# Stick-breaking attention on one Trainium2 core: the values as stationary operand in two column tiles, the output row turned back by one product

## What is computed

```
# SB_HEADS = 8, SB_DIM = 64, SEQ = 2048, Q_BLOCK = 128
def stick_breaking_block(q, k, v, q_pos, k_pos):
    z = jnp.einsum('bhtd,bhsd->bhts', q, k).astype(jnp.float32) * (SB_DIM ** -0.5)
    mask = k_pos[None, :] < q_pos[:, None]
    log_beta = jnp.where(mask, jax.nn.log_sigmoid(z), -jnp.inf)
    log_1m = jnp.where(mask, jax.nn.log_sigmoid(-z), 0.0)
    rest = lax.cumsum(log_1m, axis=3, reverse=True) - log_1m
    a = jnp.exp(log_beta + rest)
    return jnp.einsum('bhts,bhsd->bhtd', a.astype(v.dtype), v)
```

## Time and profile before

| | |
|---|---|
| median of 3 runs | 3280.84 us (3278.66 to 3281.20) |
| profiled execution: its own time | 3281.12 us |
| profiled execution: span from first to last instruction | 3279.5 us |
| PE busy, share of the span | 3177.8 us, 97% |
| DVE / ACT / POOL busy | 1542.3 / 1075.8 / 775.8 us |
| the attention phase, by its instructions | about 808 to 1334 us of the span |
| PE / DVE / ACT / POOL busy from 808 to 1336 us | 518.8 / 459.4 / 374.9 / 333.4 us |

### The profile page before, as it was taken

The page is one execution under the profiler, slowest core; times in us unless marked ns, Lnnn a source line. Parts: engine busy times, 40 slices in busy tenths (PEclk is TensorE's granted clock), DMA queues, the critical chain, the costliest instruction groups (busy, mean ns, idle before and its releaser), DMA issues.

```text
span 3279.5 us, 45289 instructions
## 1 busy us (share of the span) xinstructions
PE 3177.8 (97%) x17258; PEld 2794.3 (85%) x17258; DVE 1542.3 (47%) x1979; ACT 1075.8 (33%) x2073; POOL 775.8 (24%) x688
## 2 busy tenths in 40 slices
PE   7999999898999999899999999999999999999998
PEld 3878887677998999777879999999999998887886
DVE  2300016531988899676665444344444445324321
ACT  3611112222776777323554212222122123213110
POOL 2421112320665666211111111111111114002000
PEclk9999999998999999899999999999999999999999
DMA  5322224332622240476554111111111115435332
GB/s 187 110 70 73 70 77 136 121 119 87 158 54 54 54 92 18 156 244 222 186 174 147 52 52 52 52 34 44 52 52 52 43 34 200 164 128 169 120 132 60
DMA packets 250868, 336.08 MB, mean 102 GB/s; under 512 B 58652, under 2 KB 170840, under 8 KB 243932
## 3 DMA queue, kind: packets, MB, share of 16 engines
q1 hardware_dynamic: 234526, 284.75, 28.6%
q0 software_dynamic: 14864, 49.31, 4.5%
q10 hardware_dynamic: 1332, 0.06, 0.0%
HBM read 225.16 MB, written 108.89 MB: 102 GB/s over the span
## 4 chain that ended last, share of the span: by engine, by line
PE 55%; DVE 2%; issue 1%; ACT 0%; SPq 0%; DMA 0%; POOL 0%; DVEq 0%; ACTq 0%; POOLq 0%
PE facc L1971 29%; PE dacc L1997 15%; PE eacc L1951 5%; PE mpm L2025 2%; PE mpT L2017 1%; PE mpD L2008 1%; PE eyT L1935 0%; PE mpN L2051 0%; PE exT L1964 0%; PE mpT L2066 0%; PE mpN L2055 0%; PE mpS L2035 0%; DVE fV L1742 0%; DVE fV L1738 0%; DMA mRU<-ug_d 0%
## 5 line engine op out<-in xcount | busy, mean ns | idle before, releaser
L1971 PE MATMUL facc<-fh,fwH 128*128 128x416 f32 x3520 | 946.7, 350 | 0.0
L1971 PEld LDWEIGHTS facc<-fh,fwH 128*128 128x128 f32 x3520 | 659.8, 188 | 5.8 <-issue 0.3
L1971 PE MATMUL facc<-fh,fwL 128*128 128x416 f32 x1760 | 618.4, 351 | 0.0
L642 PE MATMUL pacc<-pring,h1H 128*128 128x512 f32 x1360 | 445.1, 398 | 10.2 <-POOL h1L L524 5.8
L952 POOL TENSOR_TENSOR aS<-aS,aC 128x512 f32<-128x512 f32 (+3 forms) x326 | 333.7, 1029 | 192.6 <-DVE aC L914 189.9
L914 DVE TENSOR_TENSOR_SCAN aC<-aB,aC,a 128x512 f32<-128x512 f32 (+3 forms) x326 | 362.8, 1113 | 15.7 <-ACT aB L889 8.2
L1738 DVE TENSOR_SCALAR fV<-fU,fcw,fcb 128x2048 f32<-128x2048 f32 (+2 forms) x90 | 116.3, 1334 | 526.1 <-ACT fU L1554 509.9
L1552 ACT ACTIVATE fU<-facc 128x416 f32<-128x416 f32 (+1 forms) x220 | 113.0, 515 | 755.3 <-PE facc L1971 755.3
L1997 PE MATMUL dacc<-dfreed 128*128 128x512 f32 (+1 forms) x1380 | 327.5, 395 | 6.3 <-DVE dfreed L1785 3.8
L1971 PEld LDWEIGHTS facc<-fh,fwL 128*128 128x128 f32 x1760 | 330.3, 188 | 1.5
L1429 POOL TENSOR_TENSOR fwL<-fraw,fwH 128x1024 fp32r<-128x1024 f32 x44 | 134.6, 3063 | 815.0 <-ACT fwH L1543 815.0
(11 more groups left out here) (275 smaller groups left out, 4220.0 us busy)
## 6 DMA issues: line engine op xcount, KB each, us to landing
proj_out<-pstage SPq DMA_DIRECT2D x119, 256.0 KB, 2.0
dfreed_plain<-act_d SPq DMA_DIRECT2D x20, 1408.0 KB, 6.5
fraw<-w_up SPq DMA_DIRECT2D x44, 512.0 KB, 5.5
act_d<-fV SPq DMA_DIRECT2D x21, 1024.0 KB, 5.3
qk_T<-pturn POOLq DMA_DIRECT2D x68, 256.0 KB, 3.1
mwa<-w_ada SPq DMA_DIRECT2D x16, 1024.0 KB, 5.6
dthird_plain<-act_d SPq DMA_DIRECT2D x11, 1408.0 KB, 6.4
praw<-w_in SPq DMA_DIRECT2D x56, 256.0 KB, 2.8
```

Of the source, the lines that this page charges most:

```text
L642: op = mm_(acc[:, n % NB], h[:, kk, tok(t)], weight(q, w), start=(kk == 0 and part == 0), stop=(kk == KD - 1 and part == 2))
L1971: mm = nc.tensor.matmul(dst, a[:, j, kk], b[w][:, kk], start=(kk == 0 and m == 0), stop=(kk == KD - 1 and m == 2))
```

## The change

Five edits, all in `attention`:

1. In `av` the operands of a prompt item change places. The values (128 keys x 64) are stationary, the transposed weights (128 keys x 128 queries) moving, and the result is the transposed row: 64 dimensions on partitions, 128 queries in columns. Even key blocks go to partitions 0 to 63 of the bank, odd ones to partitions 64 to 127, that is, to the left and the right half of the array's columns.
2. For each row ACT copies that 128x128 result (for i = 0 its upper half) to SBUF, tile aOT (`copy_out`, item n-7), and PE multiplies it with `pair`, two 64x64 identities one below the other (`turn_out`, item n-8). The product adds the halves and turns the row back to queries on partitions, in other columns of the same bank.
3. DVE's copy to aof waits for that product, and stands two steps later (n-9).
4. In heads 1 to 7 the rows come in the order 15, 0, 14, 1, ... 8, 7; in head 0 in the old order. The waits for a head's loads are put at the head's first row, whichever it is (`leads`).
5. The pipeline has two more steps at its end.

```diff
--- before.py
+++ after.py
@@ -711,7 +711,10 @@
     nc, d = k.nc, k.d
     W4, NPB1 = 4, NPB + 1
     PROMPT, SAMPLE, KEYS, QUERIES = range(4)
-    heads = [[(PROMPT, h, i, g) for i in range(NPT) for g in reversed(range(i // W4 + 1))] for h in range(SH)]
+    mixed = [i for pair in zip(reversed(range(NPT)), range(NPT // 2)) for i in pair]
+    order = [list(range(NPT))] + [mixed] * (SH - 1)
+    place = [{i: n for n, i in enumerate(rows)} for rows in order]
+    heads = [[(PROMPT, h, i, g) for i in order[h] for g in reversed(range(i // W4 + 1))] for h in range(SH)]
     PER = len(heads[0])
     aside = [(QUERIES, 0, 0, 0)] + [(KEYS, b, 0, 0) for b in range(NPB1)]
     for n, item in enumerate(aside):
@@ -731,6 +734,7 @@
     qk_in = [k.sem("qk_loaded0"), k.sem("qk_loaded1")]
     first_in = [k.sem(f"first_qk_loaded{n}") for n in range(NPT // 4)]
     v_in = [k.sem("v_loaded0"), k.sem("v_loaded1")]
+    out_copied, out_turned = k.sems("out_copied", "out_turned")
     (edge_set, nought_set, z_ready, pass_ready, stop_ready, left_ready, w_ready, turned, av_done, o_taken, past_k_in, past_v_in,
      sample_set, sample_stored) = k.sems(
         "edge_set", "nought_set", "z_ready", "pass_ready", "stop_ready", "left_ready", "weight_ready", "weight_turned",
@@ -746,6 +750,8 @@
         C = sbuf(nc, s, "aC", [P, RC, SEQ + 1])
         A = sbuf(nc, s, "aA", [P, RA, W5])
         of = sbuf(nc, s, "aof", [P, RO, SD])
+        OT = sbuf(nc, s, "aOT", [P, 2, P])
+        pair = sbuf(nc, s, "apair", [P, SD])
 
         xq = sbuf(nc, s, "bxq", [P, W5])
         xk = sbuf(nc, s, "bxk", [P, NPB1, W5])
@@ -780,7 +786,12 @@
 
         def prompt_row(n):
             kind, h, i, g = items[n]
-            return h * NPT + i
+            return h * NPT + place[h][i]
+
+        def leads(n):
+
+            kind, h, i, g = items[n]
+            return kind == PROMPT and top(n) and place[h][i] == 0
 
         def part(ring, depth, n):
             return ring[:, rank[n] % depth, 0:width(n)]
@@ -799,7 +810,7 @@
             if 0 <= n < N:
                 op(n)
 
-        steps = range(-4, N + 7)
+        steps = range(-4, N + 9)
 
         @block.sync
         def _(sp):
@@ -853,7 +864,7 @@
             load(1)
             for m in last_of:
                 kind, h, i, g = items[scored[m]]
-                if kind == PROMPT and i == 0 and 0 < h < SH - 1:
+                if kind == PROMPT and place[h][i] == 0 and 0 < h < SH - 1:
                     load(h + 1)
                 store(scored[m])
                 if kind == PROMPT and (h, i) == (0, NPT // 2):
@@ -896,9 +907,19 @@
             def take_even(n):
                 if n % 2 == 0:
                     take(act, lambda to, at: nc.scalar.activation(to, at, ACT.Copy), n)
+            def copy_out(n, m):
+                kind, h, i, g = items[n]
+                if not last(n) or kind != PROMPT:
+                    return
+                act.wait_ge(av_done, m + 1)
+                r = row(n) % 2
+                at_least(act, out_turned, prompt_row(n) - 1)
+                used = slice(0, SD if i == 0 else P)
+                nc.scalar.activation(OT[used, prompt_row(n) % 2], O[used, r, 0:P], ACT.Copy).then_inc(out_copied, 1)
             for n in steps:
                 scores(passing, n + 2)
                 scores(stopping, n + 2)
+                scores(copy_out, n - 7)
                 every(take_even, n - 4)
 
         @block.vector
@@ -921,21 +942,23 @@
             def out(n, m):
                 if not last(n):
                     return
-                dve.wait_ge(av_done, m + 1)
                 kind, h, i, g = items[n]
                 if kind == PROMPT:
                     p = prompt_row(n)
+                    dve.wait_ge(out_turned, p + 1)
                     at_least(dve, stored[p % RO], 16 * (p // RO))
-                    v.tensor_copy(of[:, p % RO], O[:, row(n) % 2, 0:SD]).then_inc(o_taken, 1)
+                    v.tensor_copy(of[:, p % RO], O[:, row(n) % 2, 2 * P:2 * P + SD]).then_inc(o_taken, 1)
                 else:
+                    dve.wait_ge(av_done, m + 1)
                     v.tensor_copy(ofs[:, h], O[:, row(n) % 2, 0:4 * SD]).then_inc(o_taken, 1)
             v.memset(nought[:], 0.0).then_inc(nought_set, 1)
+            v.tensor_tensor(pair[:], c["ident"][:, 0:SD], c["ident"][:, SD:P], ALU.add).then_inc(nought_set, 1)
             dve.wait_ge(nought_set, 1)
             dve.wait_ge(edge_set, 1)
             for n in steps:
                 scores(passed, n)
                 every(take_odd, n - 4)
-                scores(out, n - 7)
+                scores(out, n - 9)
 
         @block.gpsimd
         def _(pool):
@@ -961,7 +984,7 @@
                     b = h % 2
                     if top(n) and h == 0 and i % W4 == 0:
                         pe.wait_ge(first_in[i // W4], 96)
-                    elif top(n) and i == 0:
+                    elif h > 0 and leads(n):
                         pe.wait_ge(qk_in[b], 96 * ((h + 1) // 2))
                     at_least(pe, stop_ready, m - NZ + 1)
                     for half in range(2):
@@ -1002,18 +1025,37 @@
                     at_least(pe, o_taken, r - 1)
                     if kind == SAMPLE:
                         pe.wait_ge(past_v_in, 32)
-                    elif i == 0:
+                    elif leads(n):
                         pe.wait_ge(v_in[h % 2], 16 * (h // 2 + 1))
                 weight = part(A, RA, n)
                 for j, b in enumerate(blocks(n)):
-                    value = V[:, h % 2, b] if kind == PROMPT else vs[:, b, h * 4 * SD:(h + 1) * 4 * SD]
-                    mm = nc.tensor.matmul(O[:, r % 2, 0:SD if kind == PROMPT else 4 * SD], weight[:, j * P:(j + 1) * P], value,
-                                          start=(top(n) and j == 0), stop=(g == 0 and j == len(blocks(n)) - 1),
-                                          skip_group_check=True)
+                    if kind == PROMPT:
+                        e = b % 2
+                        lead = g == (i - 1) // W4 and j == 1 if e else top(n) and j == 0
+                        mm = nc.tensor.matmul(O[e * SD:(e + 1) * SD, r % 2, 0:P], V[:, h % 2, b], weight[:, j * P:(j + 1) * P],
+                                              start=lead, stop=(g == 0 and j >= len(blocks(n)) - 2), skip_group_check=True)
+                    else:
+                        mm = nc.tensor.matmul(O[:, r % 2, 0:4 * SD], weight[:, j * P:(j + 1) * P],
+                                              vs[:, b, h * 4 * SD:(h + 1) * 4 * SD], start=(top(n) and j == 0),
+                                              stop=(g == 0 and j == len(blocks(n)) - 1), skip_group_check=True)
                 mm.then_inc(av_done, 1)
+
+            def turn_out(n, m):
+
+                kind, h, i, g = items[n]
+                if not last(n) or kind != PROMPT:
+                    return
+                p = prompt_row(n)
+                pe.wait_ge(out_copied, p + 1)
+                if p == 0:
+                    pe.wait_ge(nought_set, 2)
+                used = slice(0, SD if i == 0 else P)
+                nc.tensor.matmul(O[:, row(n) % 2, 2 * P:2 * P + SD], OT[used, p % 2], pair[used], start=True, stop=True,
+                                 skip_group_check=True).then_inc(out_turned, 1)
             for n in steps:
                 every(turn, n - 3)
                 scores(z, n + 4)
+                scores(turn_out, n - 8)
                 scores(av, n - 6)
```

## The result

The changed kernel takes 3299.49 us (median of 4 runs, 3298.05 to 3300.74) against 3279.75 us before (4 runs): ratio 1.0061, 95% interval 1.0049 to 1.0073. That is 20 us slower, on the forecast's side and inside its range, where the forecast's sum has 51. The granted clock is 0.99 in the attention's window as before, the 2.4 GHz level.

What follows compares the result with a forecast made beforehand. The prediction took PE to bound the attention; items 15, turning product 17 and 2, waits 16 and longer tail 1 sum to +51 us on 3281.1, giving 3332 us, range 3275 to 3425.

Steps and rivals of the forecast that it cites:

- PE bounds the phase: Attention: PE busy 518.8 of 528 us sets its length, down to about 459 us, where DVE would.
- The swap alone gains nothing: Av with swapped operands, record behind record: 2176 records at 0.108 us, 235 us against 232 today.
- The halves overlap: Av: the two column halves stream at the same time, 152 us of slots, 80 less than today.
- full overlap within the order of issue: Av: a block's second record runs beside the other half's first; 5 slots for four blocks, 1408 slots in all.
- 0.294 us for a change of shape there and back: Each of 320 av items pays 0.145 us on the way in and 0.149 out, 94 us together.
- The turning product, 17 us, and 2 for its 64-row cases: Edit turning rows back on PE: 128 products at 0.13 us, +17; eight with 64 rows change shape again, +2.
- The 32 waits, 16 us: Av behind single-item rows waits for DVE's copy of row r-2: 0.5 us stall, 32 times, +16 us.
- The order of rows, 0: Same items in another order; PE waited 4 us for DVE in all, so 0 us gained.
- no overlap: Rival, av: the halves don't stream together, 235 us of slots in place of 152, +83: 3415 us; chance 0.22.
- no price for the shape: Rival, av: 64 columns count as the full shape, so -44 us: 3237 us, faster; chance 0.14.
- half the price: Rival, av: drained but loads not bare, 0.294 falls to 0.18, -36 us: 3296 us; chance 0.10.
- the likeliest case: Attention: halves overlap and each change of shape is paid: 3332 us, own range 3307 to 3357; chance 0.52.

Runs made afterwards that it cites:

- the fastest: Changed kernel with av for two items every second step, rows turned back at that step's start, ACT's copy behind its av: 3252.66 us, ratio 0.9913.
- the small product alone: Kernel before, plus one product of 64 stationary and 8 moving columns ahead of each prompt item's av: 3398.29 us, ratio 1.0358.

## Why the prediction was right and wrong

- **PE bounds the phase:** right. Every kernel here moved with PE's work or PE's waits, and DVE's busy time stayed near 459 us (451 in the fastest).
- **The swap alone gains nothing:** right; with one half an item costs 1.02 us against 0.84.
- **The halves overlap:** right, and 0.108 a slot as well. **The slots were miscounted; this is the step that failed:** "full overlap within the order of issue ... 5 slots, 0.54 us, and 2, 3, 4 slots for 1, 2, 3 blocks". Measured: 4 slots for four blocks (0.44 us), 4 for three, 2 for two, 2 for one. In all 224 x 4 + 32 x (2 + 2 + 4) = 1152 and not 1408, 256 x 0.108 = 28 us less. The sum of 51 becomes 23, against 19.7 measured. The assumed order of starts is the fault: it gives five slots in the changed kernel and seven with the blocks in the other order, and both take four.
- **0.294 us for a change of shape there and back:** right. The changed kernel shows 0.09 at both ends and 0.05 for each bare load; with the small product alone it is 0.37 against an estimate of 0.40.
- **The turning product, 17 us, and 2 for its 64-row cases:** 50.5 us stand in its groups; 12 of them are the way into the new shape (128 x 0.09) and 14 waits, so 24 are its own. The next load comes 0.20 us after its second record starts, 0.11 and the 0.09 of the change, where the sum took 0.056 for that record from the streaming. That the load of its 128 columns sets the 0.11 fits, but isn't shown.
- **The 32 waits, 16 us:** the size right (14 by distances between starts, 12.3 in the list of waits), the mechanism half right: with the product moved alone some 10 of the 14 us stayed, held by the place of DVE's copy.
- **The rest of the sum:** with the slots put right it has -13 for the items, 19 for the product and 16 for the waits. The distances give -19, 24 and 14. The items' 6 us are about the 7 us of waits between av and the transposes, which the sum had at nothing and which went with the change (no run shows why); they and the product's 5 cancel, so 23 lies nearer to 19.7 than its terms deserve.
- **The order of rows, 0:** right with the swap; without it the order saves 4.5 us.
- **The rivals:** no overlap was tested and is 108 us dearer; no price for the shape is excluded by the rows and by the product alone; half the price likewise. The measured 3299 lies within 4 us of that last rival's 3296, and that is luck: its mechanism isn't there. It lies below the likeliest case's own range of 3307 to 3357, so only the wider range, drawn for other mechanisms, holds it. The faster side was nearer than its chance said, since the miscounted slots are half of what it needed.

The Trainium skill ("TensorE: Matmul & The Clock Gate", The mechanism) says that matmuls start and end strictly in program order. The five slots assumed the same. Here the measurement differs, if the records reach PE in the order in which the kernel issues them, which no run here shows: with the order even, even, odd, odd an item takes four slots, and in-order starts would need seven.

## What to carry to other kernels

A stationary operand of 64 columns in fp32 has two prices here: its streaming, which the two column halves shared fully in both orders of issue, and a change of the array's shape on the way in and out, 0.29 us, which is paid for each visit and not for each matmul. So first count the visits: gather the small-shape work of several steps, and only then judge the swap. A full-shape product moved next to such a visit pays too: the turning product cost more behind av than behind the scores, and that ate what the move won. And when a producer comes later, look at what stands behind its consumer on that engine before pricing the move: ACT's copy took 29 us of PE's time that way, and the kernel with ACT's copy moved, and the product early, has them back.

## What the hardware showed that I had not expected

Records of the two column halves start 7 ns apart (13 ns with the blocks in the other order), and four records issued ahead for one half didn't hold the other (0.588 and 0.595 us an item in the two orders of issue). One fp32 product of 8 moving columns costs a saturated PE 0.37 us, nearly half of a four-block item of the kernel before, if its stationary operand has 64 columns between ones of 128. And idle from a change of shape has no releaser: the profile books it as "issue" on the weight loads, 46.2 us in 268 pieces ahead of the transposes, about half of which PE still streams.
